# Filler products in gated linear attention: eight products of constants ahead of each direction's keys and of the products from the states

## What is computed

```python
def _gla_chunked(q, k, v, logg, s0):          # per head; chunks of 64 tokens
    b = cumsum of logg inside each chunk
    def step(s, inp):
        qd = qc * exp(bc);  kd = kc * exp(-bc)
        att = where(mask, qd @ kd.T, 0.0)                       # inside the chunk
        o = qd @ s + att @ vc
        s = s * exp(bl) + (kc * exp(bl - bc)).T @ vc            # the state moves on
```

## Time and profile before

| | |
|---|---|
| median of 3 runs | 2891.81 us (2891.16 to 2892.12) |
| the profiled execution | 2892.21 us, its span 2890.3 us |
| mean granted TensorE clock | 0.985 of full speed |
| TensorE busy, share of the span | 96% |
| VectorE, ScalarE, GpSimd busy | 45%, 35%, 7% |
| gated linear attention | about 594 to 684 us of the span |

### The profile page before, as it was taken

How to read it: one execution, slowest core, us unless ns; L and a number is a source line. 1 busy time by engine, 2 the same in 40 slices (tenths; PEclk the granted TensorE clock), 3 DMA queues, 4 the chain that set the end, 5 groups by cost and what they waited for, 6 DMA issues and landing times.

```text
span 2890.3 us, 42099 instructions
## 1 busy us (share of the span) xinstructions
PE 2788.7 (96%) x18536; PEld 2454.3 (85%) x18536; DVE 1290.8 (45%) x1635; ACT 1022.7 (35%) x1289; POOL 193.0 (7%) x182
## 2 busy tenths in 40 slices
PE   6999999978999999999999989999999999989998
PEld 5787878757877878877788789999999999978998
DVE  3333333375432334323336555555555554564554
ACT  3222223332321223322224344443634444443443
POOL 1000010010000001000001000011010010133100
PEclk9999999988999999999999999999999999999999
DMA  6444344410443434344434224555435555653452
GB/s 236 143 141 159 129 142 140 161 45 31 138 145 126 159 110 153 131 134 142 136 113 139 71 73 150 185 193 164 146 130 178 176 175 174 201 138 102 133 197 79
DMA packets 398181, 406.22 MB, mean 141 GB/s; under 512 B 7216, under 2 KB 397056, under 8 KB 397872
## 3 DMA queue, kind: packets, MB, share of 16 engines
q1 hardware_dynamic: 398000, 403.54, 42.4%
HBM read 402.38 MB, written 1.12 MB: 140 GB/s over the span
## 4 chain that ended last, share of the span: by engine, by line
PE 89%; DVE 6%; ACT 4%; issue 1%; DMA 0%; SPq 0%; POOL 0%; ACTq 0%; DVEq 0%; POOLq 0%
PE bank L96 88%; DVE w_lo L107 1%; ACT w_hi L103 1%; PE bank L99 1%; DVE tmp L115 1%; ACT x_hi L103 1%; DVE gla_att L107 1%; ACT L103 0%; DMA w_raw<-in_ada_w 0%; DVE gla_st L115 0%; DVE df_sc L124 0%; SPq L133 0%; ACT df_e L104 0%; DVE acc L121 0%; DVE gla_ls L118 0%
## 5 line engine op out<-in xcount | busy, mean ns | idle before, releaser
L107 DVE TENSOR_TENSOR w_lo<-w_raw,w_hi 128x2048 fp32r<-128x2048 f32 (+2 forms) x331 | 694.0, 2099 | 937.4 <-ACT w_hi L103 936.7
L96 PE MATMUL bank<-x_hi,w_hi 128*128 128x256 f32 (+1 forms) x3128 | 1033.5, 330 | 14.5 <-DVE w_lo L107 7.9
L96 PE MATMUL bank<-x_lo,w_hi 128*128 128x256 f32 (+1 forms) x3128 | 1023.8, 327 | 0.0
L96 PE MATMUL bank<-x_hi,w_lo 128*128 128x256 f32 (+1 forms) x3128 | 1023.3, 327 | 0.0
L103 ACT ACTIVATE w_hi<-w_raw 128x2048 fp32r<-128x2048 f32 (+2 forms) x331 | 579.1, 1753 | 587.0 <-PE bank L96 229.3
L96 PEld LDWEIGHTS bank<-x_hi,w_hi 128*128 128x128 f32 x3128 | 597.4, 191 | 80.5 <-issue 31.1
L96 PEld LDWEIGHTS bank<-x_hi,w_lo 128*128 128x128 f32 x3128 | 597.5, 191 | 50.6
L96 PEld LDWEIGHTS bank<-x_lo,w_hi 128*128 128x128 f32 x3128 | 597.5, 191 | 49.6 <-issue 0.7
L96 PE MATMUL bank<-hid_hi,w_hi 128*128 128x512 f32 (+1 forms) x1056 | 357.2, 338 | 1.3 <-ACT ada_rows L103 1.3
L96 PE MATMUL bank<-hid_hi,w_lo 128*128 128x512 f32 (+1 forms) x1056 | 355.1, 336 | 0.0
L96 PE MATMUL bank<-hid_lo,w_hi 128*128 128x512 f32 (+1 forms) x1056 | 355.1, 336 | 0.0
(11 more groups left out here) (237 smaller groups left out, 2282.6 us busy)
## 6 DMA issues: line engine op xcount, KB each, us to landing
w_raw<-in_ffn_w_in SPq DMA_DIRECT2D x88, 1024.0 KB, 5.6
w_raw<-in_ada_w SPq DMA_DIRECT2D x72, 1024.0 KB, 9.2
w_raw<-in_ffn_w_up SPq DMA_DIRECT2D x44, 1024.0 KB, 5.0
w_raw<-in_attn_w_in SPq DMA_DIRECT2D x36, 1024.0 KB, 4.9
w_raw<-in_ffn_w_out SPq DMA_DIRECT2D x32, 768.0 KB, 4.7
w_raw<-in_ret_w_in SPq DMA_DIRECT2D x24, 1024.0 KB, 5.1
w_raw<-in_ffn_w_out SPq DMA_DIRECT2D x32, 640.0 KB, 4.3
w_raw<-in_odd_w_in SPq DMA_DIRECT2D x12, 1024.0 KB, 4.9
```

The costliest lines, as they stand in the source:

```text
L96: return Issued(self.eng and self.eng.matmul(out, lhsT, rhs, start=start, stop=stop, skip_group_check=loose))
L107: return Issued(self.eng and self.eng.tensor_tensor(out, a, b, op))
```

## The change

Two lines are added. Ahead of the keys of each pair and direction (six places), and in `pe_gla_heads` behind the taking of its two banks and ahead of the products (three places), TensorE does eight products of constants whose result nobody reads: 72 products, 144 records. Each of the nine calls takes one more bank in turn, so that a pair takes 17 banks and the last 15.

```diff
@@ pe_even, -1000,6 +1000,7 @@
     for m in range(3):
         for d in range(2):
+            pe_keep_busy(e, 8)
             pe_keys(e, t, m, d)
             pe_inside(e, t, m, d)
             pe_states(e, t, m, d)
```

## The result

The changed kernel takes 2900.91 us (median of 7 runs, 2900.32 to 2902.49); the kernel before, on the same chip in the same job, 2893.17 (7 runs, 2891.16 to 2893.87). The ratio is 1.0029, with an interval of 1.0017 to 1.0041: 7.7 us slower. The forecast was 2897.3, +5.5 us, within 0.2%; the time lies in the range, but the change itself, 0.27%, lies on the far side of the 0.2% that I had drawn. Of the 3.6 us between forecast and time, 1.4 is the kernel before, whose median was 2893.17 in this job and 2891.81 in the runs that I started from.

A forecast was written before the change was run, and what follows sets the result against it. TensorE, busy for 96% of the span, was taken to bound the kernel, with a relay of engines inside the stage. Terms 1.8 + 3.2 + 1.0 + 0 − 0.5 = +5.5 us on 2891.8 gave 2897.3 us, range 2892.7 to 2902.2.

The forecast's parts named there:

- Part 1: Ahead of the first keys: TensorE is the chain at full clock, nothing covers the filler, +1.8 us.
- Part 2: Ahead of the first keys of pairs two and three, behind the squares: filler mostly in slow time, 1.6 each, +3.2 us.
- Part 3: Outputs of pair three: filler and bank wait on TensorE's chain, 0.65 us without the slow stretch, taken as +1.0 us.
- Part 4: Five fillers, ahead of d = 1 keys and in outputs of pairs one and two: hidden, 0 us.
- Part 5: The tail: same work shifted, nearly all slow before, so −0.5 us, between −2 and +1.
- the fillers keep the clock up: Rival: squares, keys, inside products of pairs two and three and pair three's outputs run fast; +1.2 us, 2893.0; chance 0.15.
- the fillers run slow and shorten nothing: Rival: behind the squares of pairs two and three, slow stretch 6.8 us or more; +9.7 us, 2901.5; chance 0.22.
- the banks bind: Rival: d = 1 states wait for banks, outputs of pairs one and two come late; +9.5 us, 2901.3; chance 0.06.

The follow-up runs named there:

- 24 in the gaps: Kernel before plus 24 constant products behind the products from the states in pairs one and two, none of the change's fillers: 2890.80 us, ratio 0.9993.

## Why the forecast was right, and where not

**Part 1, +1.8:** the filler took 1.79 us in the changed kernel, where A grew by 1.60; with this filler alone A grew by 1.75. Right.

**Part 2, +3.2:** it measured 2.27 + 2.60 = 4.9. This is the term that was mis-sized; C came to 7.13 and E to 7.46, above the 6 to 7 us written down. The step that failed is the last one, where I took 1.6 each instead of my own 2.1 and 1.9 because the shorter idle "can end the slow stretch sooner". It ended later: 628.45 − 622.92 = 5.5 us behind the squares' start in pair two, and some 6.3 (659.17 − 652.90) in pair three, where before it was 5.11 and 4.71. The whole filler, 3.55 us, ran slow in both. Alone, the two cost 3.3 and 3.2, near my upper end of 3.5. Why the slow stretch lasted longer stays open; it came about with 4.07 and 4.88 us of idle ahead of the squares, less than before, so that my reason for 1.6 has nothing for it in these traces. The Trainium skill (TensorE: Matmul & The Clock Gate, Part 1) has the warm-up as a budget of time and not of matmuls; the term by that rule, 4.0, was nearer to the measured 4.9 than mine. The slow time behind the start of the squares wasn't the same each time, though: 4.7 to 7.8 us in the traces of before, after and the two fillers alone.

**Part 3, +1.0:** F grew by 0.79, where I had 0.65 with the slow stretch gone. Against a fast F of 13.66 it is 2.4 us more: 1.8 for the filler and 0.6 for the states waiting for the bank, which the turns alone cost too (15.92 against 15.29). 1.6 of this came back as the slow stretch left. The size and the wait for the bank are right. The reason that I gave for the slow stretch going, a shorter idle ahead of it, isn't shown: the kernels with the first filler alone, the two behind the squares alone and 24 in the gaps have no filler in these outputs, and it was gone there as well (F 13.65 to 13.66). That it fell elsewhere in the changed kernel is in part luck.

**Part 4, 0:** right inside the stage (B 22.85 and D 22.85 as before, no gap at `gla_r`). The idle ahead of the squares fell to 4.07 and 4.88 us, as forecast (some 4). The count of bank turns stopped at the stage's end; past it lay a wait of 2.15 us that the change misses only because its turns are nine.

**Part 5, −0.5:** G fell by 1.20. Right in sign, within its bounds; it hangs on where the slow stretches fall, which I couldn't forecast.

The stage's own terms sum to 6.1 against my 5.5, which is closer than the parts are: part 2 was 1.7 us short, and A, F and G came out 0.2, 0.2 and 0.7 us lower than I had them. The remaining 1.6 us of the measured 7.7 weren't traced to a place; they lie within what executions of one kernel differ by. With part 2 at 4.9 the sum would have been 7.2 and the forecast on the right side of 0.2%. Of the rivals, the one that the fillers keep the clock up was wrong for this placing. That the fillers run slow and shorten nothing was half right: the whole filler was slow, and the mean loss of 2.4 us per pair is past the 1.75 that I had set as its mark, but the slow stretch ended after 5.5 and 6.3 us, short of its 6.8, and the outputs of pair three were fast. That the banks bind cost nothing in pairs one and two, where this rival had it; a bank does bind past the stage in two other kernels.

## What to carry to other kernels

A filler pays only if it stands in front of the wait, in time in which the engine would idle; behind the wait it sits on the chain, and here, after idle time, it ran at the low clock, 3.55 us for 1.78. In front of it, eight products cost nothing and gained nothing. To gain, fill the idle nearly to its end (2.08 us left lost the gain of one pair, eight more products brought it back), all through the stage, into columns of a bank that is held anyway. A helper that takes a bank shifts every later bank: count the turns past the stage, up to the next place that takes several at once.

## What the hardware showed that I had not expected

How little idle was left where the clock stayed up. With every idle stretch filled, 0.29 to 1.07 us of idle ahead of the squares went with a clock of 1.00, and with 2.08 us the squares were slow from the start. With the two gaps alone filled, the clock fell 1.6 and 2.0 us behind the start of the squares, after 1.34 us of idle and after 0.56 us; why it fell after 0.56 there and not after 1.07 in the other kernel stays open. Filling all idle took the mean clock of the profiled run from 0.985 to 0.993 and its time down by 0.3%.

And where the slow stretches fall changes the time of stages that an edit doesn't touch: two executions of the same kernel differed by 3.3 us in one attention stage with every other stage equal to 0.2 us, and kernels whose first change lay at 594 us or later differed from before by up to 2.8 us in the same stage. Effects of two or three us are read here from cut stages, not from medians.
